# Shifted copies of a convolution's input by way of DRAM, and one table set for logarithm and exponential

## What is computed

```python
def rms_norm(x, g):
    xf = x.astype(jnp.float32)
    y = xf * lax.rsqrt(jnp.mean(xf * xf, axis=-1, keepdims=True) + RMS_EPS)
    return (y * g.astype(jnp.float32)).astype(x.dtype)

def conformer_conv_module(h, w_pw1, b_pw1, w_dw, b_dw, ln_g, ln_b, w_pw2, b_pw2):
    a, g = jnp.split(h @ w_pw1 + b_pw1, 2, axis=-1)
    u = a * jax.nn.sigmoid(g)
    u = causal_depthwise_conv(u, w_dw) + b_dw
    u = jax.nn.silu(layer_norm(u, ln_g, ln_b))
    return u @ w_pw2 + b_pw2

# layers a, b:  h = h + rms_norm(mixer(rms_norm(h))); h = h + rms_norm(ffn(rms_norm(h)))
# layers c, d:  h = h + mixer(rms_norm(h));           h = h + conv_ffn(rms_norm(h))
# layer c: each of 8 heads is normed (over its 128 values) and multiplied by silu(gate)
# the result is rms_norm(h)
```

## Time and profile before

| | |
|---|---|
| time, median of 3 runs | 2577.41 us (2575.49 to 2577.82) |
| the profiled execution's own time | 2577.43 us |
| its span, first to last instruction | 2575.6 us |
| TensorE busy | 2465.2 us (96%), mean granted clock 0.968 |
| DVE, ACT, POOL busy | 1263.3, 857.5, 1003.6 us |
| DMA | 213.90 MB, mean 83 GB/s |

### The profile page before, as it was taken

One profiled execution on the slowest core, in us unless ns is written; L12 is line 12 of the kernel. 1 busy time (PEld: TensorE's weight loads), 2 busy tenths in 40 slices (PEclk: granted clock), 3 DMA queues, 4 the chain that ended last, 5 costly groups with the idle time before them and its releaser, 6 DMA issues.

```text
span 2575.6 us, 31030 instructions
## 1 busy us (share of the span) xinstructions
PE 2465.2 (96%) x11202; PEld 1951.3 (76%) x11202; DVE 1263.3 (49%) x1588; ACT 857.5 (33%) x1228; POOL 1003.6 (39%) x416
## 2 busy tenths in 40 slices
PE   8999899999797889999989999999999999999997
PEld 6777688888553668888768887878888677788886
DVE  4453644411523464440166665577721666677701
ACT  5433422222411442222252254333322554333322
POOL 3223444444443244444444222344444212444443
PEclk9999899999899989999989999999999889999999
DMA  4112233333243123333322111333333111333332
GB/s 147 58 49 74 66 98 96 93 97 94 65 111 109 58 66 98 96 94 96 93 68 89 50 42 49 91 97 96 93 96 93 61 37 50 95 94 96 98 94 78
DMA packets 68386, 213.90 MB, mean 83 GB/s; under 512 B 13008, under 2 KB 13520, under 8 KB 68304
## 3 DMA queue, kind: packets, MB, share of 16 engines
q1 hardware_dynamic: 68016, 212.41, 27.4%
q10 hardware_dynamic: 288, 0.36, 0.0%
HBM read 201.79 MB, written 2.10 MB: 79 GB/s over the span
## 4 chain that ended last, share of the span: by engine, by line
PE 53%; issue 28%; POOL 10%; DVE 3%; SPq 2%; DMA 1%; ACT 1%; POOLq 0%; DVEq 0%; ACTq 0%
PE bank L454 17%; PE bank L456 17%; PE bank L455 17%; POOL w_lo L394 10%; SPq L363 2%; DMA raw<-weights_dram 1%; DVE h L1409 1%; PE bank L660 1%; DVE bz L1648 0%; DVE u_lo L1391 0%; PE bank L645 0%; PE bank L716 0%; PE bank L653 0%; ACT w_hi L970 0%; POOL m L411 0%
## 5 line engine op out<-in xcount | busy, mean ns | idle before, releaser
L394 POOL TENSOR_TENSOR w_lo<-raw,w_hi 128x1024 fp32r<-128x1024 f32 x376 | 939.6, 2505 | 1520.2 <-ACT w_hi L970 1520.1
L454 PE MATMUL bank<-u_hi,w_hi 128*128 128x512 f32 x1952 | 780.5, 400 | 21.1 <-DVE u_lo L1391 17.3
L455 PE MATMUL bank<-u_lo,w_hi 128*128 128x512 f32 x1952 | 772.0, 395 | 0.0
L456 PE MATMUL bank<-u_hi,w_lo 128*128 128x512 f32 x1952 | 771.4, 395 | 0.0
L970 ACT ACTIVATE w_hi<-raw 128x1024 fp32r<-128x1024 f32 x378 | 395.2, 1056 | 984.0 <-PE bank L456 863.0
L454 PEld LDWEIGHTS bank<-u_hi,w_hi 128*128 128x128 f32 x1952 | 374.8, 192 | 112.6 <-DVE u_lo L1391 23.1
L456 PEld LDWEIGHTS bank<-u_hi,w_lo 128*128 128x128 f32 x1952 | 373.6, 191 | 80.0
L455 PEld LDWEIGHTS bank<-u_lo,w_hi 128*128 128x128 f32 x1952 | 374.4, 192 | 78.0 <-issue 1.2
L456 PE MATMUL bank<-hid_hi,w_lo 128*128 (+1 forms) x704 | 280.9, 399 | 0.0
L455 PE MATMUL bank<-hid_lo,w_hi 128*128 (+1 forms) x704 | 277.4, 394 | 0.0
L454 PE MATMUL bank<-hid_hi,w_hi 128*128 (+1 forms) x704 | 276.0, 392 | 0.0
(11 more groups left out here) (277 smaller groups left out, 2553.7 us busy)
## 6 DMA issues: line engine op xcount, KB each, us to landing
raw<-weights_dram SPq DMA_DIRECT2D x378, 512.0 KB, 3.5
bz<-bz SPq DMA_DIRECT2D x128, 67.5 KB, 2.0
h<-x_t_dram SPq DMA_DIRECT2D x8, 256.0 KB, 6.6
out_dram<-m SPq DMA_DIRECT2D x8, 256.0 KB, 2.2
ap<-select_dram SPq DMA_DIRECT2D x1, 512.0 KB, 9.0
vec<-vectors_dram SPq DMA_DIRECT2D x1, 343.0 KB, 8.2
cmask<-masks_dram ACTq DMA_DIRECT2D x1, 224.0 KB, 2.4
bwv<-vectors_dram SPq DMA_DIRECT2D x12, 8.0 KB, 1.9
```

Of the source, the lines that this page charges most:

```text
L394: pool.tensor_tensor(w_lo[:, j, :], raw[:, j, :], w_hi[:, j, :].bitcast(F32), ALU.subtract)\
L454: pe.matmul(out, wh, xh, start=start, stop=False)
L455: pe.matmul(out, wh, xl, start=False, stop=False)
L456: return pe.matmul(out, wl, xh, start=False, stop=stop)
```

## The change

Two edits, independent of each other.

1. `shift_gated`: before, 16 DMAs copy from `bz` to `bz4` within SBUF, 32 partitions x 540 elements each. Now one DMA stores the chunk of `bz` (128 x 544) to a DRAM scratch `gated_dram`, SyncE waits until it has landed, and four DMAs load from it, 32 partitions x 4 groups x 540 each. The bytes that go to `bz4` are the same. DVE may overwrite a buffer of `bz` when its store has landed, where before it waited for the copies.
2. `log_table` is now a load of the set `natural_log_exp_and_others` and no Ln of one element. That set holds Ln and Exp, and the norm of a head gets such a load in front too. The one place that used the set before (norm of the long convolution, b_var) is as it was.

```diff
-LANDED = 16 * GROUPS * SHIFTS
+LANDED = 16 * SHIFTS
...
+        bz_kept = sem("bz_kept")
+        gated_dram = nc.dram_tensor("gated_dram", (CONV_RING, P, PADDED), F32).ap()
...
@@ shift_gated (SyncE)
-                for g in range(GROUPS):
-                    for i in range(SHIFTS):
-                        sp.dma_start(bz4[32 * i:32 * i + 32, b, g, :], bz[32 * g:32 * g + 32, b, i:i + REACH])\
-                          .then_inc(bz4_landed[b], 16)
+                sp.dma_start(gated_dram[b], bz[:, b, :]).then_inc(bz_kept, 16)
+                sp.wait_ge(bz_kept, 16 * (c + 1))
+                for i in range(SHIFTS):
+                    of = gated_dram[b].rearrange("(g p) t -> p g t", p=32)[:, :, i:i + REACH]
+                    sp.dma_start(bz4[32 * i:32 * i + 32, b, :, :], of).then_inc(bz4_landed[b], 16)
...
@@ ACT
-            def log_table(n):
+            def log_table():
 
-                act.activation(spare[:, n:n + 1], ones[:, 0:1], ACT.Ln)
+                act.preload_act_table_set("natural_log_exp_and_others")
...
             def head_norm(hd):
+                log_table()
...
@@ gated (DVE)
-                        dve.wait_ge(bz4_landed[n % CONV_RING], LANDED * (n // CONV_RING))
+                        dve.wait_ge(bz_kept, 16 * (n - CONV_RING + 1))
```

More of the change, by code:

```diff
@@ L142, in build @@
         small = sb("small", [P, 64], F32)
-        spare = sb("spare", [P, 16], F32)
         rs_tok = sb("rs_tok", [P, TT], F32)
@@ L1059, in feed_forward @@
                         pair(i, b)
-                log_table("abcd".index(l))
+                log_table()
             def way_back(l, half):
@@ L1083, in _ @@
             act.wait_ge(consts_made, 2)
-            log_table(4)
+            log_table()
             act.wait_ge(gain_landed, 16)
@@ L1149, in _ @@
                     act.activation(acat_hi[:, 4 + hd // 2, :], bank[3][:, :], ACT.Copy).then_inc(oh_ready, 1)
-            log_table(6)
+            log_table()
             square_out("a_out", "a_post")
@@ L1183, in _ @@
                     act.activation(bshift[:, :], STAT[:, :], ACT.Copy, scale=1.0 / P).then_inc(shift_ready, 1)
-            act.preload_act_table_set("natural_log_exp_and_others")
+            log_table()
             for c in range(KC - CONV_LAG - 2, KC):
@@ L1199, in _ @@
                     act.activation(dst, by[:, c, :], ACT.Silu, bias=col("ln_b", c), scale=col("ln_g", c)).then_inc(done, 1)
-            log_table(7)
+            log_table()
             square_out("b_out", "b_post", lambda n: col("b_pw2", n))
@@ L1255, in _ @@
                 if g:
-                    log_table(8)
+                    log_table()
                 for far in range(2):
```

## The result

| | us |
|---|---|
| before, median of 4 runs beside it | 2577.26 (2575.49 to 2577.82) |
| changed, median of 4 runs | 2516.89 (2514.07 to 2519.59) |
| ratio changed / before | 0.9767, 95% interval 0.9750 to 0.9784 |
| span of the profiled execution | 2517.8 (before 2575.6) |

The kernel is 60.4 us faster. One number further down needs a word: of the kernel dram16 the profiled execution was disturbed (3507.4 us at a granted clock of 0.646), so only its queue's rows are read, and its time is that of the other runs. The experiments were timed in four groups, each beside the kernel before, whose median was 2576.91, 2576.36, 2576.47 and 2574.63 us: a difference of 2 us between kernels of different groups is not read as one.

What follows compares the result with a forecast made beforehand. TensorE, busy 96% of the span, was taken as the bound, so time is won only where it idles or runs at its lower clock: 2577.4 - 30.2 (copies) - 16.7 (table loads) = 2530.5, so 2530 us, range 2521 to 2545.

Steps and rivals of the forecast that it cites:

- The copies: Convolution stage, end of slot 5 to end of last group: 143.0 us becomes 112.8, saving 30.2 us, bounds 22 and 31.
- 1.3 to 2.5 us to spare: Convolution's last chunk: its copies land this long before TensorE ends the two groups in between; the tightest margin.
- TensorE sets the round throughout: Convolution: the loop of copies and weights falls from 18.2 us to 12.9 to 14.2, below TensorE's round of 18.11.
- The heads of the gated recurrence: Head loop: DVE waits four times for Ln, load, Exp; one load goes from each, 5.2 us, bounds 2.6 and 7.
- last heads, c_fpre, d_fpre, final: Last four heads 1.3 us, feed-forward norms of the second block's two layers 3.75, final norm 1.3.
- Post norms of a and b: Four post norms TensorE idles for: one load removed from each, 4 x 1.28 = 5.1 us.
- Loads counted at nothing: Loads at a_pre, b_pre, c_pre, d_pre, first block's feed-forward norms, forget gate, first softmax: taken as covered, 0 us.
- More than computed: Rival: shorter gaps keep TensorE's upper clock in head loop and behind norms; another 8 to 12 us, about 2520; chance 0.08.
- The drain behind each load: Rival: a removed table load frees twice its 1.28 us, ACT being held behind it; about 2514 us, chance 0.02.
- The trip through DRAM is longer: Rival: landings 5 us longer leave waits at L730 and before the last group; 2540 us, chance 0.19.
- the idle before the first product stays 2.06: Sign at each post norm: TensorE's idle time stays 2.06 us but starts 1.28 earlier.
- waits for rs_head shrink by 1.3 each: Sign in the head loop: each of DVE's waits for rs_head gets 1.3 us shorter.

Runs made afterwards that it cites:

- dram16: Changed kernel with sixteen loads of 32 rows out of the DRAM scratch instead of four of 128: 2540.92 us.
- trip_twice: Changed kernel with each gated chunk stored to DRAM twice, one store after the other, ahead of the four loads: 2533.31 us.
- cd_old: Changed kernel with Ln's table alone loaded ahead of the last four head norms and at the ends of layer c's and d's feed forward: 2530.20 us.
- ab_old: Changed kernel with Ln's table alone loaded ahead of a_post, a_fpost, b_post and b_fpost, as before the change: 2524.64 us.
- warm_heads_before: Kernel before with six products of no use ahead of level products 3, 4 and 5 of the second head group: 2573.48 us, ratio 0.9989.
- warm_fill: Changed kernel with products of no use in TensorE's idle time behind the four post norms, 9 of them in the long wait: 2516.70 us.
- stall_exposed_after: Changed kernel with four of POOL's subtractions in the head loop held back until rs_head is there: 2523.32 us.

## Why the prediction was wrong

- **The copies, 30.2 us: right.** 30.7 measured, the stretch 112.8 us to the tenth. The store landed as taken (2.1). The issues were dearer in the sum than in fact (0.6 against 0.44), and the landing of the loads was taken too short (2.7 against 4.6, and up to 6.7). So the margin, "1.3 to 2.5 us to spare", was not there: the last trip took 10.1 us and left 0.40 of idle time. The prediction's estimate of 7.2 us for it, by the Trainium skill, DMA: Bandwidth & Descriptors, section Anatomy of one DMA, was short too; that section is about DMAs that GpSimd issues, and these are SyncE's. The sentence that TensorE sets the round throughout was wrong as well: the queue is behind until its last turn (a turn of it measured 14.7 us, where 12.9 to 14.2 were taken), and what it is held longer adds up over the turns (trip_twice).
- **The step that failed: "The heads of the gated recurrence ... One load goes from each, and DVE carries the gain along, 4 x 1.3 = 5.2"**, bounds 2.6 and 7. It measured 11.4. The load's own 1.28 was right. But the wait of 4.04 us that it sat in and DVE's stall by POOL belong to one ring, and with the ring shorter the stall moved from DVE's work into what is left of the wait: 1.9 and 1.7 us more in the two later rounds, nothing in the first, and 3.3 behind the last read. The stalled L1769 stood in the timeline of DVE, 2.38 for 0.42, and was not read.
- **The other step that failed, by 7.0 us: last heads, c_fpre, d_fpre, final, 6.35: 13.3.** The waits were sized by the idle time of TensorE. At the two feed forwards more than that came back (2.6 and 2.2 for 1.93 and 1.82), and 1.5 us of slower matmuls behind each of three waits were left out, as the one trace didn't have them. In cd_old's trace these make it 12.0; that the runs pay the 4.5 us of slower matmuls is likely and not shown by their times.
- **Post norms of a and b, 5.1: 7.7**, with 1.28, 1.26 and 1.27 of the Exp loads seen at a_post, a_fpost and b_fpost in ab_old's trace, the rest in small pieces behind them (0.6 at a_fpre, 1.4 at b_fpre).
- **Loads counted at nothing:** right at the start (-1.0 within its runs), not at a_fpre and b_fpre, by the same 0.6 and 1.4 in one trace.
- **The rivals.** "More than computed", about 2520 and held at 0.08, came true in size; of its cause, the clock in the head loop, warm_heads_before shows a full clock and a round no shorter, and behind the norms warm_fill shows no gain. What there is of it lies at the waits of c and d. The drain behind each load (the Trainium skill, ScalarE: Activation LUTs, What ACT_TABLE_LOAD costs) would give 2514, which is near the result by accident: in the kernel before the Exp follows its load by 0.02 us, in the changed one the Ln of a head norm follows its own by 0.01, and undoing the loads at the start costs nothing. "The trip through DRAM is longer" is what trip_twice built: 2533 where the rival said 2540. In the changed kernel itself the trip was longer than taken and left only the 0.40 us.
- **What should show it:** 25 loads, yes; no idle time above 0.5 us in the stretch, yes; the idle times at w_lo gone, yes; "the idle before the first product stays 2.06", no, 1.37; "waits for rs_head shrink by 1.3 each", only the first did.

Of the 20.2 us of busy time that TensorE lost, 7.2 are the convolution's (119.6 to 112.4), 6.1 those of the head loop and the last heads (94.1 in 1498.2 to 1600.0 of the kernel before, 88.1 in 1459.1 to 1548.7 now), and 4.2 lie right behind a_post and b_post (1.4 and 2.8). In the head loop and behind the norms the experiments found no time won by a higher clock alone, so busy time lost there is not itself a gain.

## What to carry to other kernels

When a wait is shortened in a ring of engines, read the whole ring for one turn and look at each instruction that is longer than its kind: a stall that hides in the wait, or falls just beside it, moves when the wait does. Before a low clock is priced, ask who waits for TensorE there; where nobody does, as in the head loop and behind the post norms, a higher clock won nothing that the runs could tell, and where TensorE sets the pace a wait of 2 us cost 3.5 in the traces that had the slower matmuls. A queue in a ring that starts behind has to catch up: time added to its turn adds up until it has, so a margin worked out for one chunk alone says too little.

## What was unexpected of the hardware

- One GpSimd subtraction (128x1024, 2.35 to 2.8 us) held one VectorE instruction to 2.2 to 2.4 us for 0.41 to 0.74, and to 2.9 for 0.69 where both started together (stall_exposed_after).
- Behind waits of 1.86 to 2.10 us the granted clock was 0.66 to 0.72 over the next 5 to 6 us in cd_old's execution, and 1.00 in the kernel before's at the same places.
- Four loads of 270 KB from DRAM, one behind the other, landed 3.1 to 6.7 us after their issue (median 4.6), while a weight load of 512 KB takes 3.5.
- To issue a DMA took SyncE 0.63 to 0.69 us for SBUF to SBUF (32 partitions), 0.46 to 0.53 for DRAM to SBUF of the same shape (dram16's disturbed execution), 0.44 for 128 partitions from DRAM, 0.33 for the store.
